# Two high matmuls before two low ones at the head of each half-chunk

## The reference

```python
# layer 1: stick-breaking attention
q, k, v, g = jnp.split(h @ w_in_a, 4, axis=-1)          # 2048 x 8192
out = (o * silu(g)) @ w_out_a                            # 2048 x 2048
x = x + rms_norm(out, g_post)
x = x + (p_i @ w_ple_proj) * sigmoid(x @ w_ple_gate)     # 256 x 2048, 2048 x 2048
# layer 2: latent attention; w_dkv, w_in_b, w_uk, w_uv, w_uq, w_out_b, then the same update of x
# layer 3: differential attention beside a short convolution, then a gated feed-forward
proj = hn @ w_in_2                                       # 2048 x 6144
mix = jnp.concatenate([a, c], axis=-1) @ w_out_2         # 2048 x 2048
f = (silu(hn @ w_gate_2) * (hn @ w_up_2)) @ w_down_2     # 2048 x 5632 twice, 5632 x 2048
```

## Time and profile before

| | |
|---|---|
| median of three runs | 2170.02 us |
| the profiled execution, whole | 2173.58 us |
| its span, first to last instruction | 2171.8 us |
| TensorE matmuls busy | 2156.8 us, 99% of the span |
| TensorE weight loads busy | 1866.3 us, 86% |
| VectorE busy | 1391.3 us, 64% |
| ScalarE busy | 1155.8 us, 53% |
| mean granted clock of TensorE | 0.999 |

### The profile page before, as it was taken

One profiled execution on the slowest core, in us unless ns is written; L12 is line 12 of the kernel. 1 busy time (PEld: TensorE's weight loads), 2 busy tenths in 40 slices (PEclk: granted clock), 3 DMA queues, 4 the chain that ended last, 5 costly groups with the idle time before them and its releaser, 6 DMA issues.

```text
span 2171.8 us, 29214 instructions
## 1 busy us (share of the span) xinstructions
PE 2156.8 (99%) x12000; PEld 1866.3 (86%) x12000; DVE 1391.3 (64%) x1745; ACT 1155.8 (53%) x1529; POOL 27.8 (1%) x42
## 2 busy tenths in 40 slices
PE   9999999999999999999999999999999999999998
PEld 8888888888888888888888888888888888888887
DVE  6665555657787666577657787576656544565655
ACT  6555454555766565566545555565445444444443
POOL 1000000000010000000000000000000000000000
PEclk9999999999999999999999999999999999999999
DMA  7566666565656454566665555556666666666654
GB/s 246 172 185 174 183 171 179 169 190 179 192 161 182 137 155 151 184 200 189 189 182 167 171 169 183 186 164 186 193 187 192 191 193 192 190 192 187 208 184 150
DMA packets 223124, 393.77 MB, mean 181 GB/s; under 512 B 20905, under 2 KB 42930, under 8 KB 222864
## 3 DMA queue, kind: packets, MB, share of 16 engines
q1 hardware_dynamic: 221664, 388.35, 59.9%
q0 software_dynamic: 1184, 3.50, 0.5%
q10 hardware_dynamic: 144, 0.07, 0.0%
HBM read 389.76 MB, written 2.11 MB: 180 GB/s over the span
## 4 chain that ended last, share of the span: by engine, by line
PE 94%; DVE 4%; ACT 1%; issue 0%; DMA 0%; SPq 0%; DVEq 0%; ACTq 0%
PE ps L904 93%; DVE WL L1450 1%; PE ps L914 1%; DVE TMP L1450 0%; DVE xT L1450 0%; DVE H L1453 0%; DVE O L1453 0%; DMA XN<-in_x 0%; ACT WH L1181 0%; ACT SQ L1181 0%; ACT KEPT L1194 0%; DVE gT L1453 0%; ACT L1185 0%; ACT gT L1181 0%; DVE gT L1450 0%
## 5 line engine op out<-in xcount | busy, mean ns | idle before, releaser
L1450 DVE TENSOR_TENSOR WL<-RAW,WH 128x1024 fp32r<-128x1024 f32 (+1 forms) x733 | 887.6, 1222 | 425.5 <-ACT WH L1181 423.1
L1181 ACT ACTIVATE WH<-RAW 128x1024 fp32r<-128x1024 f32 (+1 forms) x733 | 768.4, 1055 | 664.6 <-PE ps L904 656.2
L904 PE MATMUL ps<-H,WH 128*128 128x512 f32 x3157 | 1113.4, 397 | 1.3 <-DVE WL L1450 0.6
L904 PE MATMUL ps<-H,WL 128*128 128x256 f32 x3152 | 882.3, 280 | 0.0
L904 PEld LDWEIGHTS ps<-H,WH 128*128 128x128 f32 x3157 | 591.7, 188 | 138.5 <-DVE WL L1450 2.1
L904 PEld LDWEIGHTS ps<-H,WL 128*128 128x128 f32 x3152 | 595.7, 189 | 1.4
L904 PE MATMUL ps<-O,WH 128*128 128x512 f32 (+2 forms) x1383 | 476.3, 392 | 2.1 <-DVE WL L1450 2.0
L904 PE MATMUL ps<-O,WL 128*128 128x256 f32 x1344 | 375.9, 280 | 0.0
L904 PEld LDWEIGHTS ps<-O,WH 128*128 128x128 f32 x1383 | 256.8, 188 | 60.7 <-DVE WL L1450 3.1
L904 PEld LDWEIGHTS ps<-O,WL 128*128 128x128 f32 x1344 | 253.7, 189 | 0.4
L904 PE MATMUL ps<-WH,ACTS 128*128 128x512 f32 x704 | 218.3, 390 | 0.0
(11 more groups left out here) (225 smaller groups left out, 1358.3 us busy)
## 6 DMA issues: line engine op xcount, KB each, us to landing
RAW<-in_w_in_a SPq DMA_DIRECT2D x127, 512.0 KB, 3.7
RAW<-in_w_in SPq DMA_DIRECT2D x96, 512.0 KB, 3.6
RAW<-in_w_gate SPq DMA_DIRECT2D x88, 512.0 KB, 3.9
RAW<-in_w_up SPq DMA_DIRECT2D x88, 512.0 KB, 3.9
RAW<-in_w_down SPq DMA_DIRECT2D x88, 512.0 KB, 4.8
RAW<-in_w_ple_gate SPq DMA_DIRECT2D x64, 512.0 KB, 3.8
RAW<-in_w_in_b SPq DMA_DIRECT2D x40, 512.0 KB, 3.7
RAW<-in_w_out_a SPq DMA_DIRECT2D x32, 512.0 KB, 3.6
```

Source lines behind the costliest of these rows:

```text
L904: return e.matmul(o, l, r, start=start, stop=True, skip_group_check=True)
L1181: return e.activation(o, i, f, **kw)
L1450: return e.tensor_tensor(o, x, y, op)
```

## The change

A constant `TOGETHER = 2` is added. In the usual form the low matmul of a pair is no longer issued right behind its high one. The pair is put on a list `held`; once the second pair of the half-chunk has had its high matmul, the list is emptied, which issues the low ones of both; from then on each pair's low one comes right behind its high one again. A half-chunk of four pairs becomes high 0, high 1, low 0, low 1, high 2, low 2, high 3, low 3, where it was high 0, low 0, high 1, low 1, and so on. The signals go with the low matmuls as before, in the same order. The forms with `solo` and `one` go on as they were.

```diff
+TOGETHER = 2
...
-                for j, t in order[part * len(order) // 2:(part + 1) * len(order) // 2]:
+                held = []
+
+                def lows():
+
+                    for j, t in held:
+                        b, k = g.banks[t], ks[j]
+                        m = mm(ps[:, b, S:2 * S], lo[:, j, t * P:(t + 1) * P], g.xs[:, k, 0:S])
+                        marked(m, j, t)
+                    held.clear()
+
+                def marked(m, j, t):
+                    end = j == js[-1] and t == g.nt - 1
+                    whole = last and j == js[-1] and (g.solo or t % 2 == 1 or end)
+                    names = ([("full", name, t if g.solo else t // 2)] if whole else []) + ([("used", i)] if end else [])
+                    if names:
+                        m.then_inc(*ev(dense_done, *names))
+
+                items = order[part * len(order) // 2:(part + 1) * len(order) // 2]
+                for n_, (j, t) in enumerate(items):
...
                         mm(ps[:, b, :], wh, g.xs[:, k, :], first and j == 0)
-                        m = mm(ps[:, b, S:2 * S], wl, g.xs[:, k, 0:S])
-                    end = j == js[-1] and t == g.nt - 1
-                    whole = last and j == js[-1] and (g.solo or t % 2 == 1 or end)
-                    names = ([("full", name, t if g.solo else t // 2)] if whole else []) + ([("used", i)] if end else [])
-                    if names:
-                        m.then_inc(*ev(dense_done, *names))
+                        held.append((j, t))
+                        if n_ >= TOGETHER - 1 or n_ == len(items) - 1:
+                            lows()
+                        continue
+                    marked(m, j, t)
```

## The result

| | before | after |
|---|---|---|
| median, us | 2170.09 (2169.51 to 2170.37, 4 runs) | 2183.53 (2183.33 to 2183.69, 4 runs) |
| the profiled execution, whole | 2173.58 | 2183.69 |
| its span | 2171.8 | 2181.9 |
| mean granted clock | 0.999 | 0.999 |

The changed kernel is slower: 1.0061 times before, 95% interval 1.0049 to 1.0073, or +13.4 us. The forecast was 2161, the range ended at 2182. The profiled executions differ by only 10.1 us. They run 1.8 to 2.4 us ahead of before's profiled execution by then, 1.3 to 1.6 of them in the first 98 us: so before's profiled execution took longer than the kernel does as a rule, and the medians are what to explain.

A forecast was written before the change was run, and what follows sets the result against it. TensorE was taken to bound the kernel, by the number of matmuls times the distance between starts. Losing 9.3 us of slow rhythm and adding 0.2 of waits gave -9.1 us, forecast 2161 us, range 2158 to 2182.

The forecast's parts named there:

- Matmuls, loads and signals: Whole kernel: none of the matmuls or loads added or removed, signals free banks and buffers at the same place; cost 0.
- The wait term of +0.2: Group starts: low 0 also waits for the second pair's activations or bank; bound 0 to 1.2 us, taken as 0.2.
- The account of before: Whole kernel before: 4475 undisturbed pairs average 348.74 ns, 2.07 ns over the fast rhythm, 9.3 us in all.
- the floor: Fast rhythm of 346.7 ns a pair, seen in the feed-forward; reaching it or nearly so, 2158 to 2165 us, had chance 0.38.
- The step that failed: All half-chunks: the new order settles on a cycle of eight at 2 x 346.7 ns, so the 9.3 us go.
- bounds that I had worked out: Each half-chunk against the floor: -5 to +23 ns, where before stands at +8.3.
- the slow rhythm: 353.3 ns a pair, mostly in attention parts and gate products; claimed to need strict high-low alternation, 30% of pairs.
- The rival that came true: Every half-chunk, feed-forward included: the new order never settles, +11.9 us, 2182; slower, mild or in full, had chance 0.34.
- the first term: In the slower rival, the first four matmuls of a half-chunk, high, high, low, low: +5 ns over the floor.
- the second: In the slower rival, the two pairs behind the first four matmuls run slow: +13.3 ns a half-chunk.
- The rival "the order does not matter": Whole kernel: the interruption before a stretch picks the rhythm, 0 +- 4 us, 2170; no effect or a few microseconds, chance 0.24.
- The check named for it: Feed-forward half-chunks, 1480 to 1690 us: four pairs should take 1.387 us; 1.40 or more means the slow rival.

The follow-up runs named there:

- experiments 1 and 2: Kernel before with other matmul orders in single feed-forward groups; the second also begins each group behind an extra 384-column matmul: 2175.47 and 2174.53 us, one run each.
- Experiment 5: Kernel before with one odd half-chunk, of eight kinds, in plain feed-forward groups, met from the floor and from the slow rhythm: 2176.77 us in one run.
- experiments 8 and 9: experiment 8, then the same fifteen odd half-chunks each put one half-chunk later: 2170.14 us in one run for the latter.
- experiment 8: Kernel before with HLHLHLLH in fifteen single half-chunks placed in slow stretches: 2168.57 us against 2170.96, ratio 0.9989.

## Why the prediction was wrong

**What held.** TensorE sets the time, and the distance of starts is all that moves: waits of 2.6, 1.4 and 0.5 us stand where they stood. Matmuls, loads and signals cost nothing. The wait term of +0.2 cannot be seen. The account of before was right in size: 9.3 us above the floor, read from 4475 pairs, is what the sum of +13.9 needs to meet the measured +13.4. The half-chunks are 1156 and not 1158, since two chunks of one block stand at the start and not four; that is worth 0.04 us. And the order did come to one cycle throughout the kernel.

**The step that failed** is "What is periodic must then settle on a cycle of eight; I take the floor, +0 for high, high, low, low and for the pairs behind". The first half is right (experiments 1 and 2), the second was a choice without a row, and it took the wrong end of bounds that I had worked out, -5 to +23 ns: the value is +20.0. The reason given was that the slow rhythm "needs strict alternation to live". It does not. Its six steps live on in the new order, with two matmuls put in between. An extra 384-column matmul had ended it in the earlier trace rows were read as a stream of one width that ended it; from these I concluded that any break ends it. But the earlier trace rows cannot show that: the pairs ahead of them, `fu5`, ran on the floor. Experiment 5 shows that a break switches the rhythm in both directions and that what it does depends on kind and place; experiments 8 and 9 show one and the same kind switching at one place and not at the others.

**The rival that came true** is the slower one, in full. It had 18.3 ns per half-chunk, from +5 for the first four matmuls and +13.3 for two slow pairs; the cycle has 20.0. 1158 x 1.7 = 2.0 us is the difference between its +11.9 and +13.9. By the floor prices of the first two pairs, 693.3 ns, the first four steps after are +1.6 ns over (235.7 + 226.7 + 113.3 + 119.2 = 694.9) and the two pairs behind +18.5 (711.8): the first term was too large and the second too small. It also named the place: the feed-forward, on the floor from end to end, paid 6.2 of the 13 us. Its chances, 0.34 against 0.38 for the floor, were not far off, but the rows of entry behind 512-column steps were split and no row had the new sequence, so nothing put the floor first. And the range ended at 2182, the rival's own sum, so it left out whatever lay above; 2183.5 was measured.

**The rival "the order does not matter"** fell: 346.7 to 351.7 ns a pair by order, 2170.7 and 2179.5 for two whole kernels. Its picture of an interruption that picks the rhythm was half right, for the plain order alone, as the ten pairs shown with the result say.

**The check named for it** worked: 1.40 us or more for four pairs in the feed-forward would be the slow rival, and it is 1.407.

What inside TensorE holds the rhythm stays open. The steps of slow and floor streams differ by a few ns, at most 11, with no wait in the profile, and no run here took the weight loads or the PSUM banks apart from the order. Nor was it tried to correct the two misplaced odd half-chunks of experiment 8.

## What to carry to other kernels

In a stream that waits for nothing, read the starts in nanoseconds over a whole period, and compare the same work at two places: equal work at two distances is a rhythm that the stream carries along, and an edit must be priced as a cycle, measured in one group, not as a sum of neighbours. What a group leaves behind is paid by the next ones, so what a part of such a change costs when tested alone is not what it costs in the whole. When bounds for an unknown step lie on both sides of the break-even, the value goes by rows of the same sequence or the chances stay even. And before a row is taken as the end of a rhythm, check that the rhythm was there ahead of it.

## What the runs showed of the hardware

- One order of matmuls of 512 and 256 columns in turn runs at 346.7 or 353.3 ns a pair at the same granted clock of 0.999, with no wait, and holds either for 64 pairs and more, through chunk and group boundaries. The same code at the same place ran at one in one execution and at the other in another (3.53 and 3.47 us for ten pairs).
- Four other cycles of the same eight matmuls cost 348.3 (HHLLHHLL), 350.0 (HHHLLLHL), 350.8 (HHHHLLLL) and 351.7 ns a pair (HHLLHLHL), the first and the last from either rhythm.
- One extra matmul of 384 columns in a stream without waits led to 346.7 in 10 of 10 cases. A reordered half-chunk did so or the reverse, by its kind and by where in the three-pair cycle it stood: HLHLHLLH ended the slow rhythm in 9 of 9 cases at one place, in 0 of 13 at the other two.
- Fifteen such half-chunks, with no work added, made the kernel 0.11% faster (0.02 to 0.2%), the only version here whose gain is clear of the noise.
